# A hybrid decoder step: five reorderings and a second DMA queue for the forget pages

## The reference

```python
def mixer_sample(h, past_nsa, past_fox, past_logf, win_buf, w_in, ...):
    q_n, k_c, v_c, k_s, v_s, k_w, v_w, gates, q_f, k_f, v_f, logf = project(h, w_in, b_gate, b_forget)
    kc, vc, c_end, ovl, ksb, vsb = nsa_full_keys(cat(past k_c, k_c), ..., cmp_pe, cmp_w1, cmp_w2)
    # compress: blocks of 32 tokens plus a position term cmp_pe, gelu(flat @ w1) @ w2
    ck = cumsum(cat(past_logf, logf))
    # per head: compressed, selected (top 16 blocks) and window attention, gated, for the NSA heads;
    # forget heads: softmax(q_f k_f / 8 + cq - ck) v_f over all past tokens
```

## Time and profile before

| | us |
|---|---|
| median of 3 executions | 2205.44 (2203.41 to 2209.02) |
| the profiled execution, as timed | 2206.01 |
| its span, first to last instruction | 2204.2 |
| PE busy | 1847.0 (84%) |
| DVE, ACT, POOL busy | 956.7, 585.3, 216.2 |
| granted clock of PE, mean | 0.905 of full speed |

### The profile page before, as it was taken

How to read it: one execution, slowest core, us unless ns; L and a number is a source line. 1 busy time by engine, 2 the same in 40 slices (tenths; PEclk the granted TensorE clock), 3 DMA queues, 4 the chain that set the end, 5 groups by cost and what they waited for, 6 DMA issues and landing times. The chain is left out here.

```text
span 2204.2 us, 35692 instructions
## 1 busy us (share of the span) xinstructions
PE 1847.0 (84%) x13487; PEld 1633.0 (74%) x13487; DVE 956.7 (43%) x1823; ACT 585.3 (27%) x1171; POOL 216.2 (10%) x468
## 2 busy tenths in 40 slices
PE   6999997778680899999956923999999998999993
PEld 5999995756350566666745913999999998999992
DVE  4433321205231677767766265222222212555558
ACT  4100001203120556565652222001010111333331
POOL 2000004711401111121110000000000000000000
PEclk9999996989685899999988956999999999999996
DMA  5437534626977503120003011111111110111113
GB/s 184 175 107 177 187 101 79 155 54 227 298 207 156 101 2 87 28 61 1 2 20 117 19 79 45 41 48 48 48 48 38 48 48 24 44 41 42 43 39 147
DMA packets 168640, 188.09 MB, mean 85 GB/s; under 512 B 36633, under 2 KB 135432, under 8 KB 167810
## 3 DMA queue, kind: packets, MB, share of 16 engines
q1 hardware_dynamic: 142754, 147.04, 22.9%
q0 software_dynamic: 12608, 30.87, 5.2%
q10 hardware_dynamic: 13152, 8.52, 1.8%
HBM read 151.83 MB, written 38.71 MB: 86 GB/s over the span
## 5 line engine op out<-in xcount | busy, mean ns | idle before, releaser
L163 PE MATMUL psum<-hf_hi,gu_hi 128*128 128x352 f32 x1056 | 341.5, 323 | 35.3 <-DVE gu_lo L2390 35.3
L164 PE MATMUL psum<-hf_lo,gu_hi 128*128 128x352 f32 x1056 | 339.2, 321 | 0.0
L165 PE MATMUL psum<-hf_hi,gu_lo 128*128 128x352 f32 x1056 | 338.9, 321 | 0.0
L163 PEld LDWEIGHTS psum<-hf_hi,gu_hi 128*128 128x128 f32 x1056 | 198.8, 188 | 36.4 <-issue 36.4
L164 PEld LDWEIGHTS psum<-hf_lo,gu_hi 128*128 128x128 f32 x1056 | 199.0, 188 | 0.0
L165 PEld LDWEIGHTS psum<-hf_hi,gu_lo 128*128 128x128 f32 x1056 | 198.5, 188 | 0.0
L163 PE MATMUL psum<-h_hi,down_hi 128*128 128x352 f32 x528 | 173.9, 329 | 18.9 <-DVE h_lo L2489 18.9
L163 PE MATMUL psum<-x_hi,w_hi 128*128 128x352 f32 x528 | 171.8, 325 | 6.2 <-DVE gf_nat L593 4.9
L1845 ACT ACTIVATE probs<-psum,neg_max 128x640 f32<-128x640 f32 (+7 forms) x192 | 138.0, 719 | 146.3 <-DVE neg_max L1978 142.9
L164 PE MATMUL psum<-h_lo,down_hi 128*128 128x352 f32 x528 | 172.7, 327 | 0.0
L165 PE MATMUL psum<-h_hi,down_lo 128*128 128x352 f32 x528 | 172.5, 327 | 0.0
(11 more groups left out here) (349 smaller groups left out, 3323.6 us busy)
## 6 DMA issues: line engine op xcount, KB each, us to landing
fox_ring<-in_cache_fox_kv SPq DMA_DIRECT2D x128, 256.0 KB, 3.5
zT<-z_stage SPq DMA_DIRECT2D x22, 528.0 KB, 2.9
w_ring<-in_w_in POOLq DMA_DIRECT2D x22, 512.0 KB, 5.2
gu_ring<-in_w_ffn_gate SPq DMA_DIRECT2D x22, 512.0 KB, 3.8
gu_ring<-in_w_ffn_up SPq DMA_DIRECT2D x22, 512.0 KB, 3.8
down_ring<-in_w_ffn_down SPq DMA_DIRECT2D x44, 256.0 KB, 2.6
nsa_page<-in_cache_nsa_kv POOLq DMA_DIRECT2D x64, 128.0 KB, 5.4
out<-nat SPq DMA_DIRECT2D x12, 512.0 KB
```

Source lines behind the costliest of these rows:

```text
L163: nc.tensor.matmul(dst, w_hi, x_hi, start=start, stop=False)
L164: nc.tensor.matmul(dst, w_hi, x_lo, start=False, stop=False)
L165: return nc.tensor.matmul(dst, w_lo, x_hi, start=False, stop=stop)
```

## The change

1. Stage A: `w_split` is opened at DVE's start, so that the first two weight loads are issued ahead of the x tiles; ACT's nine squares stand behind all its copies; PE turns five x tiles before the first `gates` part and the other four before the second; `spread_rstd` stands behind the first projection tile. Several semaphores are merged into three, with offsets in place of names.
2. Stage B, `position_bias`: the product has `w1` as the stationary operand and one column of `pe_cols` as the moving one, and gives a column, so that copy and turn of a row go.
3. Stage B, SP: tile 4's chunk DMA stands before the log forget DMAs, each round of which has its own counter; the first four fills stand between the two rounds of log forgets and before the end of the compression.
4. From fill 4 on, SP issues sequences 0 and 1 of each fill and POOL sequences 2 and 3; each ring slot has a counter for each queue.
5. The queries of the first head pair and the shared keys and values of stage C are loaded by SP behind its last fill, in stage B; buffers are laid out so that their space is free then.

```diff
         def _(dve):
             by_k = gains[:, 0, :].unsqueeze(2)
+            dve.sem_inc(w_split, 2)
...
             for j in range(4, 14):
                 low(j)
-            dve.sem_inc(w_split, 2)
             dve.sem_inc(z_copied, 1)
...
-            for t in range(4):
+            for t in range(5):
                 turn_x(t)
             gates(0)
-            for t in range(4, 7):
+            for t in range(5, QT + 1):
                 turn_x(t)
             gates(1)
-            for t in range(7, QT + 1):
-                turn_x(t)
             gates(2)
-            spread_rstd()
             for l in PLAN:
...
                 if l is PLAN[0]:
+                    project(0, 0)
+                    spread_rstd()
+                    project(0, 1)
+                    pair(1)
+                else:
+                    loop(pe, l["pairs"], pair)
...
-                if t == 0:
-                    act.wait_ge(ones_set, 5)
-                else:
-                    act.wait_ge(squared, t)
+            act.wait_ge(ones_set, 5)
+            for t in range(QT + 1):
+                rows = P if t < QT else S
+                if t:
+                    act.wait_ge(head_act, SQUARED + t)
                 nc.scalar.activation(square[0:rows, :], x_nat[:, t, :] if t < QT else xs_nat[:, :], ACT.Square,
...
                     for kv in range(2):
                         for t in range(CB):
-                            last = nc.tensor.matmul(psum[0:1, 7, kv * P:(kv + 1) * P], pe_cols[:, kv, t:t + 1], w1[0:DH, kv, t, :], start=(t == 0), stop=(t == CB - 1))
-                    last.then_inc(tab_done, 1)
-                    pe.wait_ge(tab_copied, 2)
-                    for kv in range(2):
-                        last = nc.tensor.transpose(psum[:, 7, kv:kv + 1], pe_row[0:1, kv * P:(kv + 1) * P], ident[0:1, 0:1])
+                            last = nc.tensor.matmul(psum[:, 7, kv:kv + 1], w1[0:DH, kv, t, :], pe_cols[:, kv, t:t + 1], start=(t == 0), stop=(t == CB - 1))
                     last.then_inc(tab_done, 1)
...
+        def fill(eng, f, sequences, done):
+
+            which, r, p = FILLS[f]
+            if f >= SLOTS:
+                kind, r0, p0 = FILLS[f - SLOTS]
+                PE.wait(eng, ("kf", r0, p0, SEQ4 - 1) if kind == "K" else ("use_v", r0, p0))
+            at = 0 if which == "K" else 512
+            for q in sequences:
+                page = page_of(eng, pages, r * SEQ4 + q, p)
+                src = a["cache_fox_kv"][0, bass.ds(page, 1)].rearrange("o p a h d -> (o p) (a h d)")
+                eng.dma_start(fox_ring[:, f % SLOTS, q, :], src[:, at:at + 512]).then_inc(done[f % SLOTS], 16)
...
                 for chunk_tile in (2, 3, 4):
                     load_chunks(chunk_tile)
-                    if chunk_tile > 2:
-                        load_lf(chunk_tile - 3)
+                load_lf(0)
+                PE.wait(sp, ("ct", 4, 1, 1))
+                for f in range(ALONE):
+                    fill(sp, f, range(SEQ4), ring_loaded)
+                load_lf(1)
                 PE.wait(sp, ("vc", 8))
                 DVE.wait(sp, ("ev", ("vc", 8)))
-                for f in range(len(FILLS)):
-                    fill(f)
+                for f in range(ALONE, len(FILLS)):
+                    fill(sp, f, (0, 1), ring_loaded)
+                PE.wait(sp, ("o_nsa", RN - 1))
+                load_queries(sp, env, 0)
+                load_shared(sp, env, nsa_kv_prompt)
...
+                    for f in range(ALONE, PAGES):
+                        fill(pool, f, (2, 3), ring_loaded_pool)
                     for r in range(RN):
                         if r == 0:
                             load_nsa(1)
+                        for f in range((2 * r + 1) * PAGES, (2 * r + 2) * PAGES):
+                            fill(pool, f, (2, 3), ring_loaded_pool)
                         DVE.wait(pool, ("ev", ("ot_nsa", r)))
...
+                        if r + 1 < RN:
+                            for f in range((2 * r + 2) * PAGES, (2 * r + 3) * PAGES):
+                                fill(pool, f, (2, 3), ring_loaded_pool)
                         DVE.wait(pool, ("ev", ("ot_fox", r)))
...
-                load_q(0)
-                for half in range(2):
-                    part = slice(half * DH, (half + 1) * DH)
-                    sp.dma_start(k_slc[part, :, :], ...).then_inc(kv_loaded, 16)
-                    sp.dma_start(k_win[part, :, :], ...).then_inc(kv_loaded, 16)
                 load_fox(0)
-                for g in range(G):
-                    sp.dma_start(v_slc[:, g], ...).then_inc(kv_loaded, 16)
-                    sp.dma_start(v_win[:, g], ...).then_inc(kv_loaded, 16)
```

More of the change, by code:

```diff
@@ L138, in program @@
             w1, chunks = early_tiles(nc, early)
+        with ExitStack() as early:
+            q_nsa, k_slc, k_win, v_slc, v_win = query_tiles(nc, early)
+        q_loaded = [sem(f"c_q_loaded{hp}") for hp in range(2)]
+        kv_loaded = sem("c_kv_loaded")
         pages_loaded, w1_loaded = sem("pages_loaded"), sem("w1_loaded")
@@ L459, in _ @@
-            act.wait_ge(squared, QT + 1)
-            nc.scalar.activation(total[:, :], total[:, :], ACT.Sqrt, bias=eps[:, 0:1], scale=1.0 / D).then_inc(rooted, 1)
+                                     accum_out=total[0:rows, t:t + 1]).then_inc(head_act, 1)
+            act.wait_ge(head_act, SQUARED + QT + 1)
+            nc.scalar.activation(total[:, :], total[:, :], ACT.Sqrt, bias=eps[:, 0:1], scale=1.0 / D).then_inc(head_act, 1)
             for part in range(3):
-                act.wait_ge(spread, part + 1)
+                act.wait_ge(head_pe, SPREAD + part + 1)
@@ L813, in build_b @@
         imp_rows = sb("imp_rows", [P, 16])
-        o_nsa = sb("so_nsa", [P, P])
-        o_nsaT = sb("so_nsaT", [P, P])
         B = Banks(B_JOBS)
@@ L1594, in pool_order, with query_tiles, sb, load_queries @@
     return names
+C_FIRST = H * 120 + 2 * 2 * 4 * DH + 2 * 2 * 4 * P
+C_QUERY = 2 * 2 * T + 2 * G * T + 2 * G * QT * DH
+def query_tiles(nc, ctx):
+    def sb(name, shape):
+        return ctx.enter_context(nc.sbuf_tensor(name, shape, F32))
+    sb("behind_mix", [P, 3 * KD * N + C_FIRST])
+    return sb("q_nsa", [P, 2, 2, T]), sb("k_slc", [P, G, T]), sb("k_win", [P, G, T]), sb("v_slc", [P, G, QT, DH]), sb("v_win", [P, G, QT, DH])
+def load_queries(sp, env, hp):
+    rows = env["zT"].rearrange("n p t -> (n p) t")
+    for e in range(2):
+        src = rows[(2 * hp + e) * DH + TILE["q_n"] * P:(2 * hp + e + 1) * DH + TILE["q_n"] * P, 0:T]
+        for half in range(2):
+            sp.dma_start(env["q_nsa"][half * DH:(half + 1) * DH, hp % 2, e, :], src).then_inc(env["q_loaded"][hp % 2], 16)
+def load_shared(sp, env, nsa_kv_prompt):
+    rows = env["zT"].rearrange("n p t -> (n p) t")
+    done = env["kv_loaded"]
+    for half in range(2):
+        part = slice(half * DH, (half + 1) * DH)
+        sp.dma_start(env["k_slc"][part, :, :], rows[(TILE["nsa_kv"] + 2) * P:(TILE["nsa_kv"] + 3) * P, 0:T].rearrange("(g d) t -> d g t", g=G)).then_inc(done, 16)
+        sp.dma_start(env["k_win"][part, :, :], rows[TILE["win_kv"] * P:(TILE["win_kv"] + 1) * P, 0:T].rearrange("(g d) t -> d g t", g=G)).then_inc(done, 16)
+    for g in range(G):
+        sp.dma_start(env["v_slc"][:, g], nsa_kv_prompt[0, 0, :, 3, g, :].rearrange("(t p) d -> p t d", p=P)).then_inc(done, 16)
+        sp.dma_start(env["v_win"][:, g], env["vw_nat"].rearrange("(t p) (g d) -> p t g d", p=P, g=G)[:, :, g, :]).then_inc(done, 16)
 def low_tiles(nc, ctx):
@@ L1645, in build_c @@
         tables_loaded, filled = sem("c_tables_loaded"), sem("c_filled")
-        kv_loaded = sem("c_kv_loaded")
-        q_loaded = [sem(f"c_q_loaded{hp}") for hp in range(2)]
         fox_loaded = [sem(f"c_fox_loaded{hp}") for hp in range(2)]
@@ L1684, in _ @@
                 sp.wait_ge(filled, 2)
-                def load_q(hp):
-                    for e in range(2):
-                        src = rows[(2 * hp + e) * DH + TILE["q_n"] * P:(2 * hp + e + 1) * DH + TILE["q_n"] * P, 0:T]
-                        for half in range(2):
-                            sp.dma_start(q_nsa[half * DH:(half + 1) * DH, hp % 2, e, :], src).then_inc(q_loaded[hp % 2], 16)
                 def load_fox(hp):
```

191 lines of the change are left out of this document (88 added, 103 removed).

## The result

| | kernel before | changed kernel |
|---|---|---|
| median | 2207.53 us (20 runs) | 2212.26 us (20 runs) |
| lowest to highest | 2203.41 to 3218.93 | 2207.66 to 2215.85 |
| profiled execution, span | 2204.2 | 2212.6 |
| mean granted clock of PE | 0.905 | 0.902 |

(One of the 20 runs of before took 3218.93 us; it is left out of the ratio.) The ratio is 1.0021, 95% interval 1.0014 to 1.0028: 0.2% slower, within the 0.3% that counts as no change. The forecast was 2183 with a range of 2171 to 2198. It was wrong by 29 us, and the range does not hold the time. It gave 0.92 to a time that is faster by more than 0.3%, and 0.05 to one within it.

What follows compares the result with a forecast made beforehand. PE was taken to bound the kernel, its idle time set by what stands ahead on the SP and POOL queues. 2206.0 + 1.5 (stage A) + 0.4 (stage B) + 1.0 (hand-over) - 26.3 (stage C) = 2182.6 us, range 2171 to 2198.

Steps and rivals of the forecast that it cites:

- The position product: Stage B: 128 passes at 0.11 us, 14 us instead of 27.46; upper end no gain, 27.5.
- the wait for fill 4: Stage B, round 0 keys: PE waits 13.4 us for SP's fifth key page, behind the log forgets of round 1.
- The hand-over: End of stage B: POOL's last stores run beside SP's 4.2 MB of loads for stage C; 1 us added, ends 0 and 5.
- cases that pay less: Rival, 0.20, 2191 to 2204: product pass stays at 0.215 us (2196), or half the 4.2 MB is in flight at stage C's start (2192).
- Value pages of round 0: Stage B, round 0 value phase: after the first page, value pages follow 2.3 us apart.
- Stage A: Head of the kernel: first tile at 41 to 46, third at 73 to 78 after some 5 us idle; 1.5 us lost.
- 33 us idle before the first value page: Stage B, round 0: PE idles about 33 us before its first value page, released by POOL's queue behind its 36 loads.
- 24.5 us to the forget scores: Head of stage C: first forget scores 24.5 us into it instead of 50.8, a gain of 26.3 us.
- the lead of the compression: Stage B: compression ends 33.5 us earlier, at 464.9, but the whole lead is gone by the end of round 0.
- two queues do nothing: Rival, no chance of its own: PE waits in both rounds as before, only stage C's loads count; 2182 us.
- slower than before: Rival, 0.04: POOL issues its pages more slowly than 1.155 us; loss meets gain at 2.1 us a page, 2213 at 2.3.

Runs made afterwards that it cites:

- change_halves: The changed kernel with only its position product put on two row halves of the array in turns: 2198.47 us, 0.9959 to before.
- early_loads_only: The kernel before plus the early loads of queries and shared operands, new position product and tile places: 2188.41 us, 0.9919 to before.
- sp_alone: The changed kernel with all forget pages issued by SP, one counter per ring slot, other reorderings kept: 2190.52 us, 0.9927 to before.
- product_halves: forgets_by_pool with keys' position product on the lower 64 array rows and values' on the upper, in turns, into two banks: 2143.21 us, 0.9713 to before.
- order_only: The kernel before plus SP's new order, new position product and tile places, all forget pages by SP: 2207.75 us, 1.0008 to before.
- forgets_by_pool: sp_alone with the log forgets of round 1 issued by POOL behind its loads for round 0: 2163.65 us, 0.9799 to before.
- two_queues_placed: product_halves with paired 512-byte value rows, and POOL issuing half of fills 8 to 11 and 24 to 31 only: 2145.62 us, 0.9723 to before.
- shared_by_pool: product_halves with the shared keys and values issued by POOL after its round 1 selected-output stores: 2152.57 us, 0.975 to before.

## Why the prediction was wrong

**The position product was the step that failed.** The prediction took 0.11 us a pass from the compressed scores, 14 us in all, and named "no gain, 27.5" as the upper end. It wrote down that the passes of that row alternate between halves of the array, and took its number all the same. On one half a pass is a weight load of 128 columns, and costs what moving 128 columns cost before: 27.43 us against 27.46. The row that was nearest in shape was not nearest in what overlaps. The Trainium skill, "TensorE: Matmul & The Clock Gate", section LDWEIGHTS (loading the stationary operand), has the time of a load go by its columns and not by its rows. The columns show here: with 64 rows each, a load of one column is recorded at 123 ns before and one of 128 columns at 330 after; that rows do not count no run here shows. Section The mechanism lets loads overlap with running products only when they are in another row group. With that the trace agrees: 0.214 us a pass on one half, 0.107 on two in turns.

change_halves shows what this did: with the product at 13.81 us, the wait for fill 4 is 14.13 (13.4 predicted), "o_nsa" ends at 520.1 (521.3) and the last value page has been read at 588.0 (predicted to be there at 585.3, and 2 to read it). To the end of round 0 the chain was right step by step, and 14 us of the miss are this one term. In the changed kernel the same chain, started late, gives 10.12, 532.6 and 601.2.

**The hand-over was mis-sized.** The term was 1 us, with an upper end of 5, and it is 8. early_loads_only has it alone: block start 8.2 us late, 27.3 us back by the forget scores, some 2 lost again behind them, 17 to 18 in all where the sum had 25.3. POOL's eight last stores, of 4 KB each, land in 1.9 to 2.9 us in the kernel before (first fence), where the DMA engines are idle (share 0.11), and in 8.5 to 9.8 behind the early loads (second). The block starts 5 to 6 us after the last has landed in both.

```profile
L953 POOL DMA_DIRECT2D oT_dram<-so_foxT x8: 622/622/622, 664.1 to 668.4; - x8
DMA to landing us min/median/max: 1.9/2.0/2.9
```

```profile
DMA to landing us min/median/max: 8.5/9.0/9.8
```

The prediction had seen that 4.2 MB run beside the stores and added 1 us for it, from no row. It also named both as cases that pay less, but each by itself, 2196 and 2192, and the second by another cause: half of the loads still in flight inside stage C. There the loads were in time (25.2 us against 24.5); the block itself began late. The two cases have one chain of work behind them and add up, to 2206 and more, and the range ended at 2198.

**Smaller.** Value pages of round 0 follow 3.0 us apart instead of 2.3, the last pages of round 1 wait 2.98 and 3.60 us for pages that run beside the early loads, so round 1 takes 1.6 us more than before where the sum had 3 less. (That sum also slips: its own rows give 4.3 us late at the end of round 0 and 2.4 back in round 1, 1.9 and not 0.4.) Two more us go behind the last value page, where PE waits 2.83 us for DVE's copy of the forget output instead of 0.88. DVE in turn waits until POOL's stores of the selected output of round 1 have landed:

```profile
DVE so_fox L1465 <- DMA oT_dram<-so_nsaT: 23.6, 1, 23.6
```

These stores stand behind POOL's value pages, so they are issued from 669.49 instead of 635.87, beside the early loads. With SP alone, or with the loads in stage C, PE's wait there is 0.9 us again. Tile 4 is turned 10.0 us after the issue of its chunks instead of 5.7; POOL's loads for round 0 run beside it. Behind the first forget scores another 3.5 us go. By 742 it is 1.2: four products with v_win take 0.70 us at 741.5, at a granted clock of 0.50, and took 0.44 at 735.8, at 1.00. Another 1.2 go where the second head pair begins: the same products take 5.9 us from 831.8 at 0.50, and took 4.6 from 825.7 at 0.68. The clock is low for longer there in early_loads_only and sp_alone too; why, and where the last us goes, is open.

**Stage A** was right in its mechanism: the first tile starts at 41.8, within 41 to 46, and the third 32 us later:

```profile
53.33 2.28 PE L383 MATMUL psum<-diag,ones 128*128 128x128 f32 x18
```

```profile
73.91 0.66 PE L167 MATMUL psum<-x_hi,w_hi 128*128 128x352 f32 x1 [4.53 <-DVE w_lo L535]
```

The idle of 4.53 us was foretold as "some 5". The taken value, 1.5 us lost, had the wrong sign: PE reaches stage B at 345.3 on average in the twelve kernels with the new head (343.3 to 346.6) and at 346.1 in the three with the old one. The difference is less than 1 us.

The prediction's first paragraph also passes over four low slices of PE between 1102 and 1377 us; the change has no part there.

**Right:** the 33 us idle before the first value page (32.15), released by POOL's queue; PE's wait for SP's fill 4; 24.5 us to the forget scores (25.2); that the lead of the compression is lost whole. The prediction asked what would be late next and found it. What it did not do was to take the second queue out of the sum: by its own rows, value pages issued by SP would not have stood behind POOL's 36 loads. That difference is the 21 us of sp_alone, and the rival "two queues do nothing" gave 2182, where sp_alone, the nearest to that case, takes 2190. The rival *slower than before* gave 2213 at 2.3 us a page, next to what was measured. That is luck: POOL issued its value pages of round 0 at 1.28 us on average, and the time was lost elsewhere.

**The balance**, all from ratios: early loads -18 (-23 to -13), new order on SP +2 (-1 to +5), stage A and the position product nothing measurable, together -16; the second queue +21; the changed kernel +5.

**A better kernel.** product_halves at 2143.21 us (0.9713 of before) beats both. It keeps the rest of the change, leaves the fills to SP, gives the log forgets of round 1 to POOL where it idles, and halves the position product.

**Open:** why the 4 KB stores need 8 us behind the early loads even when the values among these come in half as many rows; whether the early loads could run in a stretch where DMA engines idle (437 to 520 us, share 0.30 in order_only) was not tried, since their tiles lie on memory in use until "o_nsa" of round 1.

## What to carry to other kernels

Where an engine only issues transfers, its stream is a resource like PE: write down what stands ahead of the transfer that is waited for, before and after. If that sum stays the same, a reordering is worth nothing (order_only), and moving an item to a queue that idles can be worth most of its length (forgets_by_pool: 27 of 35 us). Before giving work to a second queue, write down what stands ahead of it there too: here half of the value pages stood behind 36 other loads, and that cost 21 us. No run here has a second queue that helps: where it did not stand behind other loads, the DMA engines were full or nearly so without it (share 1.04 and 0.88). When you price an operation, take a row that has the same overlap, not only the same shape, and add up misses that lie on one chain before closing the range.

## What the runs showed of the hardware

- At a granted clock of 0.5, a pass with 64x128 fp32 weights and one moving column takes 0.214 us on one row half and 0.107 when row halves alternate. One with a single weight column and 128 moving columns takes 0.214 too.
- The DMA engines give 370 to 374 GB/s in the value phase of round 0, with forget pages from SP alone and selected pages from POOL; 324 where POOL issues some of the forget pages too (two_queues_placed).
- SP issues a 256 KB page in 1.12 us with its page lookup, and a 4 KB one in 1.10 to 1.13: the length of the stream goes by the number of issues, not by the bytes.
- POOL issues each of the four loads with rows of 256 bytes in 0.9 us (shared_by_pool). SP needs 0.6, 11.4, 6.1 and 1.3 us for the same four in the changed kernel.
- Stores of 4 KB landed in 1.9 to 2.9 us alone (before) and in 8.5 to 9.8 us behind 4.2 MB of loads (early_loads_only).
